# Delta-rule recurrence in 128-token chunks: another operand layout and another job order for the triangular inverse

## The chip, the cores and the metric

The kernel runs on one core of a Trainium2 chip. The time is device microseconds (us) of one execution; of several runs the median counts. The engines are PE (TensorE: matrix products, results to PSUM; PEld is its weight load), DVE (VectorE), ACT (ScalarE), POOL (GpSimd) and SP (DMA queues). Each works through its own instruction list in order and waits on semaphores where it needs another's result.

## What is computed

One encoder layer: an input projection feeds three head groups (an RWKV-7 mixer, a 2-D neighbourhood attention, a latent attention), then an output projection, layer norms and a feed-forward block. The change touches only the recurrence of the first group, for 1024 tokens, 4 heads of 64 channels, and two directions, each a scan over all tokens:

```python
def step(S, inp):
    r_t, w_t, k_t, v_t, a_t, b_t = inp
    sa = jnp.einsum('bhvk,bhk->bhv', S, a_t)
    S_new = S * w_t[:, :, None, :] + sa[..., None] * b_t[:, :, None, :] + v_t[..., None] * k_t[:, :, None, :]
    y = jnp.einsum('bhvk,bhk->bhv', S_new if inclusive else S, r_t)
    return S_new, y
y_fwd = wkv7_scan(rh, dec_h[:, :, 0], k_dir[:, :, 0], vh, -kk, kk * a_h[:, :, 0], True)
y_bwd = flip(wkv7_scan(flip(rh), flip(dec_h[:, :, 1]), ..., False))
```

## The kernel before

The scan is done in 8 chunks of 128 tokens (`i`), for both directions (`d`) and all four heads at once. In a chunk the rows of `sa` depend on each other through a triangular 128 x 128 matrix, so its inverse is needed. The inverse is built by doubling: blocks of 2 tokens are there at once, four levels (`m` = 1 to 4) make them 4, 8, 16 and 32 wide, and two last steps make 64 and 128.

The program is a list of jobs, `PLAN`, and PE, ACT and DVE each walk through it, doing their own part of every job. So the place in `PLAN` sets the order on three engines. The jobs of the inverse, `HOPS`, each depend on the one before:

- G, GT, D, E at each level: a product of the level's mask `Lev` with the inverse, its transpose, a product with the transposed inverse `Xt`, a transpose back. ACT copies the result of G, GT and D out of PSUM; after E, DVE adds it to the inverse (L1245) and transposes that (L1250).
- The inverse is held compactly: `Xc` has only the four 32 x 32 diagonal blocks (128 x 32 a head), `Xtc` the same transposed. At each level POOL makes the masked matrices `Lev` (L628) and spreads `Xtc` to a full block-diagonal `Xt` (L639), 128 x 512 elements each.
- G5, D5 join 32-blocks to 64-blocks (32 x 32 products), G6, D6 join 64 to 128 (64 x 64 products). They read full matrices `X` and `Xt`: after the fourth E, ACT copies the blocks of `Xc` into `X`, four copies a direction (L854), and DVE spreads `Xt` once more (L1253).

Between the hops stand the other jobs: A (the triangular matrix itself; for chunk i+1, behind G5 and D5), KR and R (other masked products of keys and queries), tok and V (transposes), AV and AZ (what values and the old state bring into the chunk, each 128 x 256, added on DVE), U (inverse times their sum), Y (the output), S (the new state). `BACK`, `FRONT` and `AHEAD` say after which hop each stands: AZ, U, Y and S of chunk i-1 in the first two levels of chunk i, then tok, V, KR, AV and R of chunk i. Level jobs use PSUM banks 4 to 7, the rest a ring of banks 0 to 3.

Names of jobs and lines on PE: A L1672, KR L1679, R L1684, G L1693, GT and E L1697, D L1702, G5 L1715, D5 L1718, G6 L1730, D6 L1733, tok L1738, V L1742, AV L1747, AZ L1755, U L1761, Y L1768 to L1774, S L1781 and L1782. On DVE: A L1232 to L1243, KR L1266, R L1271, D5 L1258 and L1259, D6 L1262, S L1283 and L1287, Y L1291. On ACT: A L846, G, GT and D L849, G5 L858, G6 L864, tok L866, V, AV and U L869.

## Time and profile before

| | |
|---|---|
| median of 3 runs | 1944.28 us (1942.8 to 1944.61) |
| profiled execution | 1947.11 us, span 1945.0 us |
| mean granted TensorE clock | 0.951 |
| PE busy | 1763.7 us, 91% of the span |
| DVE, ACT, POOL busy | 827.2, 555.5, 320.7 us |
| recurrence (first product at 745.2, last output added at 1061.7) | 316 us |
| one chunk in the middle of it | 37.55 us |

All rows are of the one profiled execution, in us from the start of its span. Busy PE includes time at the lower clock, so busy time is not a fixed amount of work. Products are pipelined: the time from one row's start to the next row's start says more than the duration in a row, which includes the way through the array.

### The profile page before, as it was taken

Reading aid. Unit: us, or ns where it says so; the run is one execution under the profiler, and the core shown is the slowest. Engines: PE = TensorE matmul, PEld = TensorE weight load, DVE = VectorE, ACT = ScalarE, POOL = GpSimd, SP = SyncE. Lnnn points to the kernel's source line nnn. Section 1 sums busy time; section 2 is a strip of 40 time slices with the busy share of each in tenths; the row PEclk is TensorE's granted clock in tenths of the full one; section 3 lists DMA queues with packets and bytes.
Section 4 is the critical chain, followed back from the end, with each engine's and each line's share of the span. In section 5 each row is a group of like instructions: output and inputs, shape, how many; then the busy total and the mean of one; then the engine's idle time right before and its main releaser. Section 6 shows DMA issues by size and latency. Waiting matters only on the chain.

```text
span 1945.0 us, 22750 instructions
## 1 busy us (share of the span) xinstructions
PE 1763.7 (91%) x8988; PEld 1261.4 (65%) x8988; DVE 827.2 (43%) x1193; ACT 555.5 (29%) x1058; POOL 320.7 (16%) x263
## 2 busy tenths in 40 slices
PE   2999978789999996888888997999999999999995
PEld 2888736544444433676676444888888888888884
DVE  7224348765534426545553646211211121133555
ACT  3111167734343322433432012111111111122331
POOL 1700011146000004455452015200000000000000
PEclk8999999989999997788887998999999999999998
DMA  4310000000000000000001300411111111144333
GB/s 187 130 54 32 11 29 1 12 5 4 8 4 4 0 0 14 2 2 2 2 2 53 153 11 11 152 43 43 52 56 43 43 51 57 56 149 138 95 95 115
DMA packets 24277, 93.49 MB, mean 48 GB/s; under 512 B 2752, under 2 KB 5120, under 8 KB 23568
## 3 DMA queue, kind: packets, MB, share of 16 engines
q1 hardware_dynamic: 23744, 87.27, 13.0%
q0 software_dynamic: 464, 5.28, 0.7%
q8 instruction: 46, 0.75, 0.2%
q14 instruction: 23, 0.19, 0.0%
HBM read 79.92 MB, written 12.58 MB: 48 GB/s over the span
## 4 chain that ended last, share of the span: by engine, by line
PE 84%; DVE 9%; ACT 4%; issue 2%; DMA 1%; POOL 0%; SPq 0%; DVEq 0%; ACTq 0%; POOLq 0%
PE psum L1842 25%; PE psum L1868 12%; PE psum L1456 9%; PE psum L1597 5%; PE psum L1793 5%; PE psum L1607 5%; PE psum L1474 2%; PE psum L1556 2%; PE psum L1538 1%; PE psum L1579 1%; PE psum L1693 1%; PE psum L1519 1%; PE psum L1481 1%; DVE stats L1138 1%; PE psum L1761 1%
## 5 line engine op out<-in xcount | busy, mean ns | idle before, releaser
L1842 PE MATMUL psum<-h_hi,w_hi 128*128 128x512 f32 x704 | 275.2, 391 | 11.7 <-DVE h_lo L1336 11.7
L1842 PE MATMUL psum<-h_lo,w_hi 128*128 128x512 f32 x704 | 274.4, 390 | 0.0
L1842 PE MATMUL psum<-h_hi,w_lo 128*128 128x512 f32 x704 | 274.4, 390 | 0.0
L1369 DVE TENSOR_TENSOR arena<-psum,arena 128x1024 f32 (+1 forms) x22 | 27.0, 1225 | 391.3 <-ACT arena L914 391.3
L1842 PEld LDWEIGHTS psum<-h_hi,w_hi 128*128 128x128 f32 x704 | 132.6, 188 | 39.7 <-DVE h_lo L1336 12.0
L1842 PEld LDWEIGHTS psum<-h_lo,w_hi 128*128 128x128 f32 x704 | 132.6, 188 | 27.8 <-issue 0.2
L1842 PEld LDWEIGHTS psum<-h_hi,w_lo 128*128 128x128 f32 x704 | 132.5, 188 | 27.5
L628 POOL TENSOR_TENSOR arena<-arena,consts 128x512 f32<-128x512 f32 x64 | 80.2, 1270 | 321.9 <-ACT arena L846 321.9
L1868 PE MATMUL psum<-wd_hi,act_lo 128*128 128x512 f32 x336 | 130.7, 389 | 0.0
L1868 PE MATMUL psum<-wd_lo,act_hi 128*128 128x512 f32 x336 | 130.7, 389 | 0.0
L1868 PE MATMUL psum<-wd_hi,act_hi 128*128 128x512 f32 x336 | 130.7, 389 | 0.0
L1138 DVE TENSOR_REDUCE stats<-psum 128x1 f32<-128x1024 f32 x64 | 78.0, 1224 | 122.8 <-PE psum L1579 122.8
L1597 PE MATMUL psum<-arena 97*128 97x512 f32 x256 | 121.4, 602 | 3.2 <-DMA arena<-arena 2.2
L1607 PE MATMUL psum<-arena 128*128 128x512 f32 x256 | 120.3, 592 | 0.0
L1793 PE MATMUL psum<-arena 128*128 128x512 f32 x256 | 110.6, 592 | 0.3 <-DMA arena<-in_w_out 0.3
L1382 DVE TENSOR_TENSOR wd_lo<-arena,wd_hi 128x1024 fp32r<-128x1024 f32 x44 | 53.9, 1225 | 129.8 <-ACT wd_hi L928 129.8
L1456 PE MATMUL psum<-h_hi,w_in_hi 128*128 128x512 f32 x240 | 96.5, 402 | 11.1 <-DVEq L999 11.1
L809 ACT ACTIVATE arena<-psum 128x1024 f32<-128x1024 f32 x64 | 65.4, 1022 | 133.4 <-PE psum L1597 133.4
L914 ACT ACTIVATE arena<-psum 128x1024 f32 (+1 forms) x22 | 22.6, 1027 | 273.9 <-PE psum L1842 273.9
L1456 PE MATMUL psum<-h_lo,w_in_hi 128*128 128x512 f32 x240 | 95.7, 399 | 0.0
L1456 PE MATMUL psum<-h_hi,w_in_lo 128*128 128x512 f32 x240 | 95.1, 396 | 0.0
L639 POOL TENSOR_TENSOR arena<-arena,consts 128x512 f32<-128x512 f32 x64 | 80.0, 1270 | 70.8 <-DVE arena L1250 53.6
(265 smaller groups left out, 2895.8 us busy)
## 6 DMA issues: line engine op xcount, KB each, us to landing
arena<-in_w_down SPq DMA_DIRECT2D x44, 512.0 KB, 3.6
arena<-in_w_gate SPq DMA_DIRECT2D x22, 512.0 KB, 3.5
arena<-in_w_up SPq DMA_DIRECT2D x22, 512.0 KB, 4.6
arena<-in_w_in SPq DMA_DIRECT2D x15, 512.0 KB, 3.6
arena<-in_x SPq DMA_DIRECT2D x8, 512.0 KB, 10.1
resid_spill<-arena POOLq DMA_DIRECT2D x1, 4096.0 KB, 12.9
arena<-in_w_out SPq DMA_DIRECT2D x8, 512.0 KB, 6.2
arena<-resid_spill SPq DMA_DIRECT2D x1, 4096.0 KB, 19.5
```

Source lines behind the costliest of these rows:

```text
L628: pool.tensor_tensor(Lev[d][m % 2], Araw[i % 2][d], four_heads(cst((C_LV if d == 0 else C_LVT) + m - 1)), ALU.mult).then_inc(lev_ready, 1)
L639: pool.tensor_tensor(Xt[d].rearrange("p h (k c) -> p h k c", c=32), spread(Xtc[d]), own_block, ALU.mult).then_inc(xt_full, 1)
L809: act.activation(halves(e_ring[(kt) % NE]), psum[:, 2 * (kt % 2):2 * (kt % 2) + 2, :], ACT.Exp, scale=MLA_SCALE).then_inc(e_ready, 1)
L1138: v.tensor_reduce(g_max[:, b, t:t + 1], psum[:, g_banks, :], AX.XY, ALU.max, negate=True).then_inc(g_max_ready, 1)
L1382: v.tensor_tensor(wd_lo[b], raw_w[b], wd_hi[b], ALU.subtract).then_inc(wd_lo_ready, 1)
L1456: mm = pe.matmul(bank(2 * b + hf), w[:, P * k:P * k + P], x[k][:, cols], start=(k == 0 and n == 0), stop=(k == KT - 1 and n == 2))
L1474: mm = pe.matmul(bank(t), x[k][:, t * P:(t + 1) * P], wv_parts[k // 2][:, HALF * (k % 2):HALF * (k % 2) + HALF], start=(k == 0 and n == 0) ...
L1597: mm = pe.matmul(bank(2 * (kt % 2) + hf), kT[b][0:97, kt * P:(kt + 1) * P], qT[b][0:97, hf * HALF:(hf + 1) * HALF], start=True, stop=True)
L1607: mm = pe.matmul(bank(6 + hf), vh[b][:, kt, :], e_ring[kt % NE][:, hf * HALF:(hf + 1) * HALF], start=(kt == 0), stop=(kt == NT - 1))
L1793: mm = pe.matmul(bank(mixed_bank(t) + hf), mix[:, k, t * P:(t + 1) * P], w_out[k][:, hf * HALF:(hf + 1) * HALF], start=(k == 2), stop=(k = ...
L1842: mm = pe.matmul(bank(4 * b + 2 * n + hf), w[b][n][:, P * k:P * k + P], x[k][:, cols], start=(k == 0 and i == 0), stop=(k == KT - 1 and i ...
L1868: mm = pe.matmul(bank(2 * t + hf), x[b][:, t * P:(t + 1) * P], w[b][:, hf * HALF:(hf + 1) * HALF], start=(free is not None and i == 0), st ...
```

## The change

Four things, in the recurrence alone.

1. G5 and D5 read the compact `Xc` and `Xtc` themselves. DVE's spreading for D5 (L1253) and ACT's four copies a direction (L854) are gone. `Xc` and `Xtc` exist twice, for even and odd chunks (`Xcs`, `Xtcs`).
2. The diagonal blocks that G6, D6 and U still need in full `X` and `Xt` are copied by POOL (`own_blocks`), 12 copies of 32 x 128 elements a chunk: four that G6 waits for, four that D6 waits for, four that U waits for.
3. G6 and D6 are one job each for both directions (`TOGETHER`), and PE alternates between the directions from product to product.
4. AV and AZ become one job AX that accumulates both in one PSUM bank; ACT copies the sum to `Xs`, and DVE's addition is gone. All jobs get other places (`BESIDE`; a "-" belongs to the chunk before, a "+" to the next). A of the next chunk stands in levels 1 and 2 now, at most one job stands after a hop.

```diff
-BACK = {0: ("AZ0", "AZ1"), 1: ("U0",), 2: ("U1",), 3: ("Y0",), 4: ("Y1",), 5: ("S0",), 6: ("S1",)}
-FRONT = {7: ("tok0",), 8: ("V0", "V1"), 9: ("tok1",), 10: ("KR0",), 11: ("KR1",), 12: ("AV0",), 13: ("AV1",), 14: ("R0",),
-         15: ("R1",)}
-AHEAD = {16: ("A0",), 17: ("A1",)}
+BESIDE = {0: ("R1-",), 1: ("tok0-",), 2: ("U1-",), 3: ("A1+",), 4: ("U0-",), 5: ("Y1-",), 7: ("A0+",), 8: ("Y0-",),
+          9: ("S0-",), 10: ("V0",), 11: ("KR1",), 12: ("S1-",), 13: ("V1",), 14: ("tok1",), 15: ("KR0",), 16: ("R0",),
+          17: ("AX1",), 18: ("AX0",)}
+TOGETHER = ("G6", "D6")
...
-    jobs = named(("A0", "A1"), 0)
-    for i in range(NT):
+    jobs = [("A", 0, 0, 0), ("A", 1, 0, 0)]
+    for i in range(NT + 1):
         for n, (kind, m) in enumerate(HOPS):
-            jobs += [(kind, d, m, i) for d in range(2)]
-            if i:
-                jobs += named(BACK.get(n, ()), i - 1)
-            jobs += named(FRONT.get(n, ()), i)
-            if i + 1 < NT:
-                jobs += named(AHEAD.get(n, ()), i + 1)
-    return jobs + named(("AZ0", "AZ1", "U0", "U1", "Y0", "Y1"), NT - 1)
+            if i < NT:
+                jobs += [(kind, d, m, i) for d in range(1 if kind in TOGETHER else 2)]
+            for name in BESIDE.get(n, ()):
+                j = i + name.count("+") - name.count("-")
+                kind_d = name.strip("+-")
+                if 0 <= j < NT and not (kind_d[0] == "S" and j == NT - 1):
+                    jobs.append((kind_d[:-1], int(kind_d[-1]), 0, j))
+    return jobs
...
-XT_AT = LEV_AT
-XTC_AT = {(d, m, i): 12 * i + 2 * (m - 1) + (1 + m // 4) * d + 1 for i in range(NT) for m in range(1, 5) for d in range(2)}
-OWN_AT = {(d, i): 12 * i + 2 * d + 8 for i in range(NT) for d in range(2)}
-TURNED_AT = {(d, i): 12 * i + d + 11 for i in range(NT) for d in range(2)}
+XT_AT = {(d, m, i): 20 * i + 2 * (m - 1) + d + 1 for i in range(NT) for m in range(1, 5) for d in range(2)}
+XTC_AT = {(d, m, i): 10 * i + 2 * (m - 1) + d + 1 for i in range(NT) for m in range(1, 5) for d in range(2)}
+TURNED_AT = {(d, i): 10 * i + d + 9 for i in range(NT) for d in range(2)}
+FIRST_HALF_AT = {i: 20 * i + 12 for i in range(NT)}
+TURNED_OWN_AT = {i: 20 * i + 16 for i in range(NT)}
+OTHER_HALF_AT = {i: 20 * i + 20 for i in range(NT)}
...
+        elif kind in TOGETHER:
+            banks[job] = (4 + turn[0], 6 + turn[1])
+            turn = [1 - turn[0], 1 - turn[1]]
...
-        Xc, Xtc, Gc, G5 = ([heads4(32) for d in range(2)] for _ in range(4))
+        Xcs, Xtcs = ([[heads4(32) for d in range(2)] for n in range(2)] for _ in range(2))
+        Gc, G5 = ([heads4(32) for d in range(2)] for _ in range(2))
...
-                        computed(pool, ("D6", d, 0, i - 1))
+                        computed(pool, ("D6", 0, 0, i - 1))
                 else:
                     pool.wait_ge(xt_ready, XTC_AT[d, m - 1, i])
-                pool.tensor_tensor(Xt[d].rearrange("p h (k c) -> p h k c", c=32), spread(Xtc[d]), own_block,
+                pool.tensor_tensor(Xt[d].rearrange("p h (k c) -> p h k c", c=32), spread(Xtcs[i % 2][d]), own_block,
                                    ALU.mult).then_inc(xt_full, 1)
 
+            def own_blocks(full, compact, which, i):
+
+                for d in range(2):
+                    pool.wait_ge(xt_ready, XTC_AT[d, 4, i])
+                    rows64 = halves_of(d)[which]
+                    for at in (rows64.start, rows64.start + 32):
+                        rows = slice(at, at + 32)
+                        pool.tensor_copy(full[d][rows, :, rows], compact[d][rows]).then_inc(xt_full, 1)
+
             for i in range(NT):
+                if i:
+                    pool.wait_ge(xt_full, OTHER_HALF_AT[i - 1])
                 for m in range(1, 5):
                     for d in range(2):
                         level(d, m, i)
                     for d in range(2):
                         turned_full(d, m, i)
+                pool.wait_ge(xt_full, XT_AT[1, 4, i])
+                own_blocks(X, Xcs[i % 2], 1, i)
+                own_blocks(Xt, Xtcs[i % 2], 0, i)
+                own_blocks(X, Xcs[i % 2], 0, i)
...
-                elif kind == "E" and m == 4:
-                    taken(act, job)
-                    for p in range(4):
-                        rows = slice(32 * p, 32 * p + 32)
-                        act.activation(X[d][rows, :, 32 * p:32 * p + 32], Xc[d][rows], ACT.Copy).then_inc(x_full, 1)
...
-                    dst, src = halves_of(d)
-                    ins = act.activation(G6[d][dst].rearrange("p h c -> p (h c)"), psum[dst, b0, 0:256], ACT.Copy)
+                    for d in range(2):
+                        dst, src = halves_of(d)
+                        ins = act.activation(G6[d][dst].rearrange("p h c -> p (h c)"), psum[dst, BANKS[job][d], 0:256], ACT.Copy)
...
+                    if i >= 2:
+                        v.wait_ge(xt_full, OTHER_HALF_AT[i - 2])
...
-                    if m == 4:
-                        v.wait_ge(xt_ready, XTC_AT[d, m, i])
-                        v.tensor_tensor(Xt[d].rearrange("p h (k c) -> p h k c", c=32), spread(Xtc[d]), own_block,
-                                        ALU.mult).then_inc(xt_ready, 1)
                 elif kind == "D5":
                     dst, src = quads(d, d)
-                    v.wait_ge(xt_ready, OWN_AT[d, i])
...
-                elif kind == "AZ":
-                    taken(v, ("AV", d, 0, i))
-                    v.tensor_tensor(Xs[d].rearrange("p h c -> p (h c)"), bank(b0, 256),
-                                    AVs[d].rearrange("p h c -> p (h c)"), ALU.add).then_inc(out_v, 1)
...
-                        pe.wait_ge(x_full, 4 * (2 * i + d + 1))
+                        taken(pe, ("E", d, 4, i))
                     else:
                         taken(pe, ("G5", d, 0, i))
-                        pe.wait_ge(xt_ready, OWN_AT[d, i])
+                        pe.wait_ge(xt_ready, XTC_AT[d, 4, i])
                     for p in range(2):
                         dst, src = quads(d, p)
                         for h in range(4):
                             out = psum[dst, banks[p], 32 * h:32 * h + 32]
                             if kind == "G5":
+                                mm = pe.matmul(out, Araw[i % 2][d][src, h, dst], Xc[d][src, h, :], start=True, stop=True,
+                                               skip_group_check=True)
+                            else:
+                                mm = pe.matmul(out, Xtc[d][dst, h, :], G5[d][dst, h, :], start=True, stop=True,
+                                               skip_group_check=True)
+                elif kind in TOGETHER:
+                    if kind == "G6":
+                        taken(pe, ("D5", 0, 0, i))
+                        taken(pe, ("D5", 1, 0, i))
+                        pe.wait_ge(xt_full, FIRST_HALF_AT[i])
+                    else:
+                        taken(pe, ("G6", 0, 0, i))
+                        pe.wait_ge(xt_full, TURNED_OWN_AT[i])
+                        pe.wait_ge(xt_ready, TURNED_AT[1, i])
+                    for h in range(4):
+                        for d in range(2):
+                            dst, src = halves_of(d)
+                            out = psum[dst, banks[d], 64 * h:64 * h + 64]
+                            if kind == "G6":
                                 mm = pe.matmul(out, Araw[i % 2][d][src, h, dst], X[d][src, h, src], start=True, stop=True,
                                                skip_group_check=True)
                             else:
-                                mm = pe.matmul(out, Xt[d][dst, h, dst], G5[d][dst, h, :], start=True, stop=True,
+                                mm = pe.matmul(out, Xt[d][dst, h, dst], G6[d][dst, h, :], start=True, stop=True,
...
-                elif kind == "AV":
+                elif kind == "AX":
                     taken(pe, ("KR", d, 0, i))
                     taken(pe, ("V", d, 0, i))
                     for h in range(4):
-                        mm = pe.matmul(psum[:, b0, 64 * h:64 * h + 64], KAm[d][:, h, :],
-                                       tokv[d][:, h // 2, 64 * (h % 2):64 * (h % 2) + 64], start=True, stop=True)
-                elif kind == "AZ":
+                        pe.matmul(psum[:, b0, 64 * h:64 * h + 64], KAm[d][:, h, :],
+                                  tokv[d][:, h // 2, 64 * (h % 2):64 * (h % 2) + 64], start=(h == 0), stop=False,
+                                  skip_group_check=True)
                     if i:
                         taken(pe, ("S", d, 0, i - 1))
                     else:
                         pe.wait_ge(y_cleared, 5)
                     for hp in range(2):
                         mm = pe.matmul(psum[:, b0, P * hp:P * hp + P], At[:, 2 * d + hp, at_chunk(d, i)], Zs[d][:, hp, :],
-                                       start=True, stop=True)
+                                       start=False, stop=True, skip_group_check=True)
                 elif kind == "U":
-                    taken(pe, ("D6", d, 0, i))
-                    taken(pe, ("AZ", d, 0, i))
+                    taken(pe, ("D6", 0, 0, i))
+                    pe.wait_ge(xt_full, OTHER_HALF_AT[i])
+                    taken(pe, ("AX", d, 0, i))```

What this makes of PE's list at the end of a chunk, from the last products of level 4 into the next chunk's first level. Before:

```order
L1702 MATMUL psum<-arena 32x128 x8
L1684 MATMUL psum<-arena 128x128 x4
L1697 MATMUL psum<-consts,arena 128x128 x2
L1684 MATMUL psum<-arena 128x128 x4
L1715 MATMUL psum<-arena 32x32 x16
L1672 MATMUL psum<-arena 128x128 x4
L1718 MATMUL psum<-arena 32x32 x16
L1672 MATMUL psum<-arena 128x128 x4
L1730 MATMUL psum<-arena 64x64 x8
L1733 MATMUL psum<-arena 64x64 x8
L1693 MATMUL psum<-arena 32x128 x8
L1755 MATMUL psum<-arena 128x128 x4
```

The same place after the change (L1715 is D, L1755 tok, L1710 E and GT, L1692 KR, L1728 G5, L1697 R, L1731 D5, L1764 and L1772 AX, L1747 G6, L1750 D6, L1706 G):

```order
L1710 MATMUL psum<-consts,arena 128x128 x2
L1692 MATMUL psum<-arena 128x256 x4
L1728 MATMUL psum<-arena 32x32 x16
L1697 MATMUL psum<-arena 128x128 x4
L1731 MATMUL psum<-arena 32x32 x16
L1764 MATMUL psum<-arena 128x64 x4
L1772 MATMUL psum<-arena 128x128 x2
L1747 MATMUL psum<-arena 64x64 x8
L1764 MATMUL psum<-arena 128x64 x4
L1772 MATMUL psum<-arena 128x128 x2
L1750 MATMUL psum<-arena 64x64 x8
L1706 MATMUL psum<-arena 32x128 x8
```

A KR now stands between E and G5, an R between G5 and D5, an AX before and after G6; the two A are gone from here.

PE's list in the first level and the start of the second, before (the AZ of both directions, then U, U, Y):

```order
L1693 MATMUL psum<-arena 32x128 x8
L1755 MATMUL psum<-arena 128x128 x4
L1697 MATMUL psum<-consts,arena 128x128 x2
L1761 MATMUL psum<-arena 128x64 x4
L1702 MATMUL psum<-arena 32x128 x8
L1761 MATMUL psum<-arena 128x64 x4
L1697 MATMUL psum<-consts,arena 128x128 x2
```

After (R, tok, U and A between the hops of level 1, then G of level 2 and a U; L1779 is U, L1685 A):

```order
L1706 MATMUL psum<-arena 32x128 x8
L1697 MATMUL psum<-arena 128x128 x4
L1710 MATMUL psum<-consts,arena 128x128 x2
L1755 MATMUL psum<-consts,arena 128x128 x4
L1715 MATMUL psum<-arena 32x128 x8
L1779 MATMUL psum<-arena 128x64 x4
L1710 MATMUL psum<-consts,arena 128x128 x2
L1685 MATMUL psum<-arena 128x128 x4
L1706 MATMUL psum<-arena 32x128 x8
L1779 MATMUL psum<-arena 128x64 x4
```

Each hop is followed by one other job, and the pair of AZ at its head is no longer there.

POOL's list after the change, at the turn from one chunk to the next (L631 is `Lev`, L642 the spreading to `Xt`):

```order
L631 TENSOR_TENSOR arena<-arena,consts 128x512 x2
L642 TENSOR_TENSOR arena<-arena,consts 128x512 x2
L652 COPY arena<-arena 32x4x32 x12
L631 TENSOR_TENSOR arena<-arena,consts 128x512 x2
L642 TENSOR_TENSOR arena<-arena,consts 128x512 x2
```

Before, the list had the same pairs without the copies; the next chunk's first `Lev` now comes after all twelve.

## Rows read from the trace of the kernel before

**Rows 1.** The page: busy time by engine; 40 slices of the span, TensorE's granted clock.

```profile
PE 1763.7 (91%) x8988; PEld 1261.4 (65%) x8988; DVE 827.2 (43%) x1193; ACT 555.5 (29%) x1058; POOL 320.7 (16%) x263
PEclk8999999989999997788887998999999999999998
```

**Rows 2.** Stretches (busy us and instructions, clock, DMA), then timeline of PE at G5.

```profile
1003.40:1041.00 37.60, 32.44 (x396) 25.78 (x396) 19.80 (x55) 15.08 (x51) 19.90 (x16) 0.86 0.01 2
...
778.10 0.56 PE L1715 MATMUL psum<-arena 32*32 32x32 f32 x16 [1.40 <-ACT arena L854]
...
1041.87 0.56 PE L1715 MATMUL psum<-arena 32*32 32x32 f32 x16 [1.40 <-ACT arena L854]
```

**Rows 3.** Timeline (start, duration, engine, line, [idle before <- releaser]), end of a chunk.

```profile
1002.56 0.28 DVE L1245 TENSOR_TENSOR arena<-psum,arena 128x128 f32<-128x128 f32 x1
1002.88 2.63 ACT L854 ACTIVATE arena<-arena 32x128 f32<-32x128 f32 x8 [1.27 <-DVE arena L1245]
...
1004.32 0.56 PE L1715 MATMUL psum<-arena 32*32 32x32 f32 x16 [1.41 <-ACT arena L854]
...
1005.65 0.56 PE L1715 MATMUL psum<-arena 32*32 32x32 f32 x16 [0.77 <-ACT arena L854]
...
1010.28 1.60 PEld L1730 LDWEIGHTS psum<-arena 64*64 64x64 f32 x16 [1.56 <-ACT arena L846]
1010.31 1.76 PE L1730 MATMUL psum<-arena 64*64 64x64 f32 x16 [1.29 <-DVE arena L1259]
```

**Rows 4.** Timeline of a middle chunk: G behind the state update, D behind POOL.

```profile
991.06 0.29 DVE L1245 TENSOR_TENSOR arena<-psum,arena 128x128 f32<-128x128 f32 x1
...
991.46 0.95 PE L1693 MATMUL psum<-arena 128*32 128x128 f32 x16 [0.88 <-ACT arena L866]
991.78 2.52 POOL L639 TENSOR_TENSOR arena<-arena,consts 128x512 f32<-128x512 f32 x2 [3.62 <-DVE arena L1250]
...
994.44 0.43 PE L1702 MATMUL psum<-arena 128*32 128x128 f32 x8 [0.28 <-ACT arena L866]
```

**Rows 5.** Stretches of the recurrence, columns as in rows 2 (the clock is third from last).

```profile
757.00:768.30 11.30, 10.86 (x97) 6.33 (x100) 2.18 (x8) 5.24 (x17) 11.23 (x10) 0.50 0.01 1
...
778.90:792.20 13.30, 11.76 (x126) 10.49 (x126) 8.21 (x24) 4.95 (x16) 6.88 (x6) 0.50 0.01 2
...
1007.30:1017.50 10.20, 8.90 (x88) 7.89 (x82) 6.40 (x20) 3.05 (x10) 6.75 (x6) 0.50 0.01 2
1017.50:1044.80 27.30, 23.34 (x320) 17.72 (x320) 13.59 (x35) 11.84 (x42) 13.16 (x11) 1.00 0.01 2
1045.00:1061.50 16.50, 15.90 (x97) 13.33 (x96) 3.16 (x9) 1.79 (x5) 0.00 (x0) 0.50 0.00 1
```

**Rows 6.** Timeline: A and AZ at the low clock, KR and AV at the full one.

```profile
1007.79 0.93 PEld L1672 LDWEIGHTS psum<-arena 64*128 64x128 f32 x8
1007.79 1.23 PE L1672 MATMUL psum<-arena 64*128 64x128 f32 x8
...
1014.75 1.78 PEld L1755 LDWEIGHTS psum<-arena 128*128 128x128 f32 x8 [0.38 <-ACT arena L849]
1014.76 2.08 PE L1755 MATMUL psum<-arena 128*128 128x128 f32 x8
...
1032.35 1.14 PE L1679 MATMUL psum<-arena 64*128 64x256 f32 x8
...
1036.00 1.10 PE L1747 MATMUL psum<-arena 128*128 128x64 f32 x8
```

**Rows 7.** Groups of POOL over the whole program, shapes apart (count | busy, mean ns).

```profile
L639 POOL TENSOR_TENSOR arena<-arena,consts 128x512 f32<-128x512 f32 x64 | 80.0, 1270 | 70.8 <-DVE arena L1250 53.6 <-PE psum L1733 15.9 <-DVE arena L1243 1.3
...
L590 POOL COPY arena<-arena 64x64 f32<-64x64 f32 x64 | 18.3, 286 | 98.4 <-PE psum L1519 96.4
```

**Rows 8.** Timeline at the end of the recurrence: the last U, the last output added.

```profile
1050.63 3.61 PE L1761 MATMUL psum<-arena 128*128 128x64 f32 x16
...
1061.24 0.42 DVE L1291 TENSOR_TENSOR arena<-psum,arena 128x256 f32<-128x256 f32 x1 [3.15 <-PE psum L1774]
```

45 lines of the change are left out of this document (17 added, 28 removed).

## The prediction

> **What bounds the kernel now.** The page first [rows 1]: TensorE (PE) is busy 91% of the span, and the clock line is below 9 tenths almost only in its slices 16 to 22. That is the recurrence, 745 to 1062 us: eight chunks, two directions at once. Next the table of stretches by chunk and PE's own rows [rows 2]: PE's first G5 starts at 778.10, the last at 1041.87, and the one before it at 1004.32 [rows 3]. So a chunk takes 37.55 us in the steady part, (1041.87 - 778.10) / 7 = 37.68 on average, and in a stretch of 37.6 us PE is busy 32.44, DVE 19.80, ACT 15.08, POOL 19.90. PE is the engine to look at: 32.4 us of work and 5.1 us of waiting. Everything the diff touches lies here; the other 1630 us stay.
>
> Where are the 5.1 us? In order of time [rows 3]: G5 waits 1.41 and 0.77 for the four ACT copies of the inverse (L854, 0.33 each), and G6 waits 1.29 for the DVE copy behind D5. That is 3.5. Earlier [rows 4] G waits 0.88 because the add L1245 before it starts late, at 991.06, right behind the state update L1283 and L1287 in DVE's list, and D waits 0.28; the row names ACT there, but the POOL pair L639 ends at the same 994.30 and D needs its second result. That is 1.2. The rest, about 0.5, is the "issue" idle before a product with other row groups.
>
> Where is PE's work dearer than it need be? In the clock [rows 5]. It is at the low level (0.50, 1.2 GHz) from 1007.3 to 1017.5 and at the full one from 1017.5 to 1044.8. It falls after G5, A and D5, small products with waits between them, stays low through G6 and D6, and comes back after G, the AZ products and the first U. All seven later chunks show this with 10.2 us of low clock, the first with 13.3 [rows 5]. In those 10.2 us PE is busy 8.9; at full clock the same work would take about half, so the low stretch costs 4.4 us a chunk.
>
> **The change part by part.** *Compact inverse for G5 and D5.* The eight ACT copies and the two DVE products L1253 leave; G5 needs only the add L1245 (0.28), D5 the transpose after it (0.31). With KR0 (1.14, as L1679 [rows 6]) placed between E and G5 the 1.41 and 0.77 are covered: **-2.2**. If KR0 did not cover it, 0.3 would come back. ACT loses 2.6 us and DVE 2.2, neither of them late elsewhere.
>
> *AX1 between D5 and G6, AX0 between G6 and D6.* AX is the AV product and the AZ product in one bank, so an ACT copy and a DVE add go too (both hidden already). AX lasts 1.0 (AV) and about 0.5 (half of what one direction's AZ took at the low clock), and nearly twice that at the low one [rows 6], longer than the 1.29 wait and than the evacuation of two G6 halves (2 x 0.38): **-1.3**. What is late next is DVE's R0 mask ahead of D5's four transposes and copies (2 us together); both fit under AX1.
>
> *Own blocks on POOL.* Twelve copies of 32 x 128 elements a chunk. The trace has no such copy. Nearest rows [rows 7]: a POOL copy of 64 elements took 0.286, a POOL product of 512 elements 1.27, so 0.29 to 1.27 each; I take 0.4, near the copy. G6 needs only the first four (1.6 us after E's transpose, while PE has 5 us of KR0, G5, R0, D5 and AX1 ahead of it): nothing. All twelve take 4.8; the two level masks of the next chunk (2 x 1.27), which ran beside D5 and G6 before, now follow, and then come the two L639, which wait for D6 as before. D in the first level needs the second L639, 2.5 us after D6, and PE gets there after G, R1, GT, tok0: 2.1 at full clock, 3.5 at the low one. I take a new wait of 0.3.
>
> *G6 and D6, both directions alternating.* The 16 instructions of G6 took 1.76 at the low clock, 0.11 apiece, and their weight loads 1.60 [rows 3]; D6 the same. Their operands lie in opposite row and column halves. What alternating halves brings is shown by A, whose products alternate the two row halves: 8 loads of 128 columns in 0.93 at low clock, where AZ's 8 full loads took 1.78 [rows 6]. So between nothing and half: 0 to -1.76 for both; I take **-1.1**, near A's own busy time per product (1.23 against 2.08).
>
> The Trainium skill bears on this. TensorEngine Tiling (Array Packing), Key Properties, says that different tiles can execute LdWeights and Matmul in parallel; its 64 x 64 table would make it the full -1.76, and the chunk 0.7 shorter than I say. G6 and D6 before did not gain from that, since their four heads in a row use the same tile.
>
> *Jobs spread.* A moves from the tail, where one cost 1.23 at the low clock, to levels 1 and 2; S0 and S1 leave level 2, where S1 held up the add: **-1.2** (the 0.88 and 0.28). New thin places: no job stands between D2 and E2 (D's product and its ACT copy need about 0.9 before E can start; 0.4 is open), V1 alone between GT4 and D4 (0.3), the second direction's G a little behind its add three times (0.4), and three more changes of row group (0.5). With the 0.3 above: **+1.9**. DVE's A job (two us) now stands ahead of Y1 and Y0 in DVE's queue; both products come over 2 us later, so nobody waits. On ACT, A's copy (0.60) stands ahead of G's copy, under U0 and Y0.
>
> *Clock.* The tail has still G5, R0, D5, which are thin, so I expect one fall a chunk, later than now, around AX1. Which work brings it back? Before it was G, AZ, GT and U in a row. Now it would be G, R1, GT, tok0, D of the next first level, packed almost as tightly (in the first chunk the low level ended at 768, after V, GT, tok and D [rows 5]). I take a low stretch between the 10.2 and the 13.3 of [rows 5]: **+0.8**.
>
> Sum for a chunk: -2.2 - 1.3 - 1.2 + 1.9 - 1.1 + 0.8 = -3.1, so 34.4 us in place of 37.55.
>
> Over the program: seven periods, 7 x -3.1 = -21.7. The A jobs sit in the chunk before their own, so the last period is 1.3 shorter, and the first chunk saves its G5 wait but gets two A jobs: 0. After the last G5, now 19.8 us [rows 8] nearly all at the low clock, there are now also R0, R1, the AV part twice and a tok0 that nobody uses: +5.9 at that clock; G6/D6 and waits give back 2.4: +3.5. In all -19.5. Against the profiled execution's 1947.1 (span 1945.0) that is 1927.6; the median shown is 1944.3, 2.8 lower, so **1925**.
>
> **The rivals.** *The clock stays low through levels 1 and 2 (slower).* For it: after the last chunk PE is busy 15.9 of 16.5 us with AZ, U and Y and the clock is 0.50 all through [rows 5]; U's and Y's are just the jobs that now fill levels 1 and 2, and AZ's burst, after which the clock returned, is gone. Against it: G, R1, GT, tok0 and D stand before them. If the clock comes back only between level 3 and S0, the low stretch is 12 to 16 us longer. A low microsecond costs 4.4 / 10.2 = 0.43, so that is +5 to +7 a chunk, a chunk of 39.5 to 41.5, and 1959 to 1972. It turns the sign once the low stretch is over about 18 us.
>
> *The clock does not fall.* For it: no wait of PE in the chunk is over 0.5 us any more. Then the 4.4 and the 0.8 go, G6/D6 save only half of 1.1, and a chunk is near 30; at the end some 3 more: 1893.
> By the Trainium skill (TensorE: Matmul & The Clock Gate, the HAM clock gate) idleness throttles the clock and activity releases it; read as idleness alone, this is its case. The row against it: D6 and G ran nearly without a gap and the clock stayed low [rows 3, 5], though PE hardly idled there.
>
> *POOL becomes the bound.* If a copy costs over 0.55, the next chunk's masks and L639 come after PE; each further 0.1 is 1.2 us a chunk, and at 0.8 the gain is gone. At 1.27 a chunk would be 43 and the time 1985.
>
> *The gain is there but mostly given back*, some chunks with an early and some with a late return of the clock, or the covers thinner than I count: a chunk of 36 to 37.6, 1936 to 1947.
>
> **How the numbers follow.** My forecast (chunks of 33.5 to 35.5, 1913 to 1934) 0.50; no fall of the clock 0.13; mostly given back 0.15; low through two levels 0.17; POOL 0.05. The range must leave out no more than 0.2: from 1892, the case of no fall, to 1955, past the given-back case and up to the late return's near end; my forecast's own is 1913 to 1934. A measurement here can tell about 0.2%, 4 us, from no change: faster is 0.50 + 0.13 + 0.09 = 0.72, within it 0.07, slower 0.21.
>
> **What would show it.** Right: G5 rows without a wait for ACT, G6's wait for D5's copy gone, G6 plus D6 at 2.4 us or less for 32 instructions, DVE's A rows in levels 1 and 2, G5 to G5 at 34 to 35. The granted clock by stretch decides: one low stretch of 10 to 14 us that ends before U1 is my case; low until S0 or KR1 is the slower rival. POOL: COPY rows near 0.4 and L639 (now L642) starting just after D6. It would be wrong if those start late, or if PE's idle time in a chunk is over 3 us.

## The result, and the profile after

| | before | after |
|---|---|---|
| median | 1944.05 us (1942.8 to 1944.61, 4 runs) | 1872.72 us (1872.56 to 1874.17, 4 runs) |
| span of the profiled execution | 1945.0 us | 1870.7 us |
| G5 to G5 in the steady part | 37.6 us | 28.6 us |
| mean granted clock | 0.951 | 0.972 |

The ratio is 0.9636, 95% interval 0.9619 to 0.9652. The kernel is 71 us faster, where the forecast was 19; the time lies 19 us below the low end of the range, 1892.

The page of after, the lines that answer to [rows 1]:

```profile
PE 1722.4 (92%) x8988; PEld 1224.1 (65%) x8988; DVE 824.8 (44%) x1161; ACT 534.1 (29%) x994; POOL 348.7 (19%) x359
PEclk8999999989999998899999998999999999999998
```

There are as many products on PE as before, in 41 us less of busy time, while the whole is 74 us shorter. The dip of the clock line in slices 16 to 22 is two slices long now. The stretches of the recurrence, to be read beside [rows 2, 5] (us, then busy us and instructions of PE, PEld, DVE, ACT, POOL, then the granted clock):

```profile
741.10:765.00 23.90, 13.91 (x122) 7.92 (x122) 16.13 (x45) 6.22 (x19) 14.89 (x12) 0.53 0.01 1
...
858.30:886.90 28.60, 27.82 (x399) 21.59 (x397) 19.41 (x51) 12.22 (x42) 23.41 (x28) 1.00 0.01 2
...
972.60:986.70 14.10, 13.67 (x198) 11.68 (x196) 6.78 (x15) 4.49 (x13) 3.17 (x12) 1.00 0.01 2
```

The clock is low once in the recurrence, at its start (0.53 in the first stretch shown), and full from 766.2 to the end of the recurrence: **it does not fall in any chunk.** PE idles 0.8 us in a chunk of 28.6; before it was 5.1 in 37.6.

The timeline of the end of a chunk in after answers to [rows 3] and, for POOL, to [rows 7]:

```profile
858.28 0.89 PE L1728 MATMUL psum<-arena 32*32 32x32 f32 x32
859.11 0.71 PE L1697 MATMUL psum<-arena 64*128 64x128 f32 x8
859.75 0.93 PE L1731 MATMUL psum<-arena 32*32 32x32 f32 x32
860.61 1.10 PE L1764 MATMUL psum<-arena 128*128 128x64 f32 x8
861.55 0.66 PE L1772 MATMUL psum<-arena 128*128 128x128 f32 x4
862.20 0.68 PE L1747 MATMUL psum<-arena 64*64 64x64 f32 x16
862.81 1.10 PE L1764 MATMUL psum<-arena 128*128 128x64 f32 x8
...
867.83 0.43 PE L1715 MATMUL psum<-arena 128*32 128x128 f32 x8 [0.42 <-ACT arena L880]
...
874.72 0.52 PE L1710 MATMUL psum<-consts,arena 128*128 128x128 f32 x2 [0.27 <-ACT arena L867]
...
886.59 4.08 POOL L652 COPY arena<-arena 32x128 f32<-32x128 f32 x12 [2.28 <-DVE arena L1265]
```

G5 (L1728), R0 (L1697), D5 (L1731), AX1 (L1764, L1772), G6 (L1747) and AX0 follow one another without a wait: from the start of G5 to the start of D6 (L1750, 864.35) it is 6.1 us. Twelve POOL copies take 4.08, 0.34 each from start to start. What is left of waits are the two predicted small ones, D behind POOL's second product (0.42; the row names ACT, POOL's L642 ends at 867.69) and E behind D (0.27).

Where the 74.3 us of span came from: the recurrence starts at 743.26 instead of 745.2 (1.9); first A to first G5 29.2 instead of 32.9 (3.7); seven periods 200.1 instead of 263.8 (63.6); last G5 to the last output add 14.1 instead of 19.8 (5.7); the rest is 0.6 the other way.

### The profile page after: what moved, and what is told of

Read it like the earlier page. It is cut to its first block, busy times and chain, and to the rows that moved or that the text cites. A ratio compares the mean times of both kernels' runs of the same rounds, so it can differ in the third digit from the quotient of the medians.

```text
span 1870.7 us, 22729 instructions
## 1 busy us (share of the span) xinstructions
PE 1722.4 (92%) x8988; PEld 1224.1 (65%) x8988; DVE 824.8 (44%) x1161; ACT 534.1 (29%) x994; POOL 348.7 (19%) x359
## 3 DMA queue, kind: packets, MB, share of 16 engines
q1 hardware_dynamic: 23744, 87.27, 13.7%
## 4 chain that ended last, share of the span: by engine, by line
PE 87%; DVE 8%; ACT 3%; issue 1%; DMA 1%; SPq 0%; POOL 0%; DVEq 0%; ACTq 0%; POOLq 0%
PE psum L1860 26%; PE psum L1886 12%; PE psum L1468 9%; PE psum L1609 6%; PE psum L1811 6%; PE psum L1619 5%; PE psum L1486 2%; PE psum L1568 2%; PE psum L1550 2%; PE psum L1591 2%; PE psum L1531 1%; PE psum L1493 1%; PE psum L1710 1%; DVE stats L1152 1%; PE psum L1706 1%
## 5 line engine op out<-in xcount | busy, mean ns | idle before, releaser
L631 POOL TENSOR_TENSOR arena<-arena,consts 128x512 f32<-128x512 f32 x64 | 80.9, 1285 | 265.4 <-ACT arena L864 264.8
L1811 PEld LDWEIGHTS psum<-arena 128*128 128x128 f32 x256 | 48.3, 190 | 63.7 <-issue 59.3
```

Of the source, the lines that this page charges most:

```text
L631: pool.tensor_tensor(Lev[d][m % 2], Araw[i % 2][d], four_heads(cst((C_LV if d == 0 else C_LVT) + m - 1)), ALU.mult).then_inc(lev_ready, 1)
L1811: mm = pe.matmul(bank(mixed_bank(t) + hf), mix[:, k, t * P:(t + 1) * P], w_out[k][:, hf * HALF:(hf + 1) * HALF], start=(k == 2), stop=(k = ...
```

## The experiments

The **theory** after the result: two parts of about equal size. The waits go, as predicted, and with them goes the fall of the clock, which they had caused. The **rival**: most of the gain is order and waits, and the clock only follows. A second question is which part of the change carries it. "Period" below is G5 to G5 and "low" the time per chunk at 0.50, both in the one profiled execution. Each run has its own runs of before beside it. "Run 4" is the one told under 4.

| kernel | median, us | ratio (95%) | period | low |
|---|---|---|---|---|
| before | 1944 to 1947 | 1 | 37.6 | 10.2 |
| before, waits filled | 1957.6 | 1.0043 to 1.0085 | 38.0 to 40.4 | 3.4 to 10.2 |
| before, waits covered | 1970.4 | 1.0118 to 1.0156 | 41.0 | 17.1 |
| after, before's places | 1986.0 | 1.0142 to 1.0237 | mostly 43.5 | 20.5 |
| after, ACT copies | 1923.9 | 0.9857 to 0.9911 | 34.5 (once 35.8) | 10.2 (once 13.7) |
| after, R moved | 1905.0 | 0.9760 to 0.9813 | 29.2 to 33.3 | 0, 6.8 or 10.2 |
| after, R and KR moved | 1908.6 | 0.9779 to 0.9834 | 29.6 to 33.9 | 0, 6.8 or 10.2 |
| R moved, four products | 1896.8 | 0.9732 to 0.9762 | 30.9 | 0 |
| R moved, one product | 1886.3 | 0.9676 to 0.9742 | 29.6 | 0 |
| after, not alternating | 1877.9 | 0.9643 to 0.9675 | 29.1 | 0 |
| **after** | **1872.7** | 0.9619 to 0.9652 | 28.6 | 0 |
| after, short head | 1872.3 | 0.9609 to 0.9635 | 28.6 | 0 |
| after, warm head | 1886.7 | 0.9678 to 0.9706 | 28.6 | 0 |

**1. Filling before's waits.** The kernel before with throw-away products (128x128 by 256 columns, results unused) meant for its three waits at the end of a chunk, three ahead of the first G5, two ahead of the second, three ahead of G6:

```diff
                     if kind == "G5":
+                        filler(b0, 3 - d)
                         pe.wait_ge(x_full, 4 * (2 * i + d + 1))
...
                     if kind == "G6":
+                        if d == 0:
+                            for before in PREVIOUS["AZ", 0, 0, i]:
+                                taken(pe, before)
+                            filler(BANKS["AZ", 0, 0, i][0], 3)
```

> The kernel before with throw-away TensorE products (128x128 by 128x256, about 0.43 us each at full clock) put into its three waits: three ahead of G5 of direction 0, two ahead of direction 1, three ahead of G6. Nothing of the real work is moved or removed; no result is used. Theory 'clock': the low stretch of 10.2 us in each chunk comes from the waits and small products between level 4 and G6; with the waits filled the clock stays at the full level, a chunk goes from 37.55 to about 33 us (4.4 us less), the time to about 1909 (1900 to 1915). Rival 'waits': the time went with the waits themselves, the clock is a side effect; here all waits stay, so 1944 or up to 10 more.

It is slower, not faster. PE's timeline in it, and two rows of DVE (L1232 is A's, L1259 D5's):

```profile
935.90 1.24 DVE L1232 TENSOR_TENSOR arena<-psum,consts 32x128 f32<-32x128 f32 x4 [1.03 <-ACT arena L846]
935.91 0.71 PE L1677 MATMUL psum<-arena 64*128 64x128 f32 x8
938.18 0.28 DVE L1259 COPY arena<-psum 32x128 f32<-32x128 f32 x1
938.56 2.90 PE L1660 MATMUL psum<-consts 128*128 128x256 f32 x6 [1.94 <-DVE arena L1259]
941.39 1.60 PE L1740 MATMUL psum<-arena 64*64 64x64 f32 x16
```

The filler at G5 did its work: G5, A and D5 ran at the full clock. That ahead of G6 (L1660) filled nothing. G6 writes the bank that D5 wrote, the program waits for that bank before it comes to the filler, and the bank is free only after D5's copy (938.18 to 938.46); the filler's own bank, A's, had been read by 937.14. So all 1.94 us of G6's wait stand ahead of the filler, the clock fell in that wait (937.7), and 2.9 us of products at the low clock then stood ahead of G6. The run does not decide: the kernel before with all three waits filled was never run. It shows that with the two waits at G5 filled the one at G6 still lets the clock fall. It also gives a price. In three of its periods the low stretch is 10.2 us, in three 3.4, with the same products; they take 40.2 to 40.4 and 38.0 to 38.2, some 0.32 us for each low microsecond.

**2. The new places without the compact operands.** The kernel before with KR0, R0 and the two AV jobs between the steps, as the changed kernel has them:

```diff
-FRONT = {7: ("tok0",), 8: ("V0", "V1"), 9: ("tok1",), 10: ("KR0",), 11: ("KR1",), 12: ("AV0",), 13: ("AV1",), 14: ("R0",),
-         15: ("R1",)}
+FRONT = {7: ("tok0",), 9: ("tok1",), 10: ("V0",), 11: ("KR1",), 13: ("V1",), 14: ("R1",), 15: ("KR0",), 16: ("R0",),
+         17: ("AV1",), 18: ("AV0",)}
```

> The kernel before with another table of places only: KR0 behind E of level 4, R0 behind G5, AV1 behind D5, AV0 behind G6; A stays behind G5 and D5 (it has to, with one Xc and Xtc), AZ stays in the next level 1, the ACT copies stay. Theory 'clock': the waits of 1.4, 0.8 and 1.3 are covered and PE has real work there, the clock does not fall, a chunk is 37.55 - 3.3 - 4.4 = 30 us: about 1888 (1880 to 1900). Rival 'waits': only the 3.3 us go, 34.3 a chunk, about 1920. A third, that the compact operands are what does it: 1930 or more, since G5 still waits for ACT.

```profile
936.15 0.29 DVE L1219 TENSOR_TENSOR arena<-arena 128x128 f32<-128x128 f32 x1
936.36 0.28 DVE L1245 TENSOR_TENSOR arena<-psum,arena 128x128 f32<-128x128 f32 x1
...
938.10:979.10 41.00, 35.81 (x396) 28.45 (x397) 19.96 (x55) 15.53 (x51) 19.80 (x16) 0.79 0.01 1
...
979.12 0.84 PE L1715 MATMUL psum<-arena 32*32 32x32 f32 x16 [2.17 <-ACT arena L854]
```

(Two rows of DVE ahead of G5, the stretch of one chunk, and PE's next first G5.) G5 waits 2.17 for ACT's copies, more than the 1.41 of before, and the clock falls there; what was put behind, R, AV and A, now runs at the low clock. The wait is longer through this table itself. It puts R1 ahead of the last E, and R1's work on DVE is a mask, a reciprocal and a product (L1271, L1217, L1219); the add L1245, from which ACT copies, stands behind them and starts at 936.36, 1.5 us after E's product was out (934.88). So this table costs 25 us without the compact operands; what KR0 and R0 at G5 would have done without R1's move no run shows.

**3. The compact operands without the new places.** The changed kernel with the jobs where before had them:

```diff
-BESIDE = {0: ("R1-",), 1: ("tok0-",), 2: ("U1-",), 3: ("A1+",), 4: ("U0-",), 5: ("Y1-",), 7: ("A0+",), 8: ("Y0-",),
-          9: ("S0-",), 10: ("V0",), 11: ("KR1",), 12: ("S1-",), 13: ("V1",), 14: ("tok1",), 15: ("KR0",), 16: ("R0",),
-          17: ("AX1",), 18: ("AX0",)}
+BESIDE = {0: ("AX0-", "AX1-"), 1: ("U0-",), 2: ("U1-",), 3: ("Y0-",), 4: ("Y1-",), 5: ("S0-",), 6: ("S1-",),
+          7: ("tok0",), 8: ("V0", "V1"), 9: ("tok1",), 10: ("KR0",), 11: ("KR1",), 14: ("R0",), 15: ("R1",),
+          16: ("A0+",), 17: ("A1+",)}
```

> The changed kernel with the places of before: AX of both directions, U, Y, S of the chunk before in levels 1 and 2, R and nothing else around level 4's end, A of the next chunk behind G5 and D5. Compact operands, POOL copies, alternating G6/D6 stay. Theory 'clock': PE idles again between E, G5, D5 and G6 and the clock falls each chunk: 28.6 + 4.4 + about 1.5 of waits = 34.5 a chunk, about 1915 (1905 to 1925). Rival 'operands': the compact feed and the alternating products keep the clock up without the places; 31 a chunk or less, 1892 or less.

```profile
950.50:970.90 20.40, 16.63 (x124) 14.65 (x126) 5.79 (x19) 4.13 (x13) 10.40 (x11) 0.50 0.01 2
...
947.05 1.08 PE L1728 MATMUL psum<-arena 32*32 32x32 f32 x32
...
953.11 1.12 PE L1747 MATMUL psum<-arena 64*64 64x64 f32 x16 [2.86 <-DVE arena L1269]
955.39 1.12 PE L1750 MATMUL psum<-arena 64*64 64x64 f32 x16 [1.17 <-ACT arena L878]
```

G5 has no wait, but G6 waits 2.86 (D5's copies stand behind A's job in DVE's list) and D6 1.17, and the clock stays low for 20.5 us. This is the slower rival's price by another trigger: in the two forms tried, the places without the compact operands and these without the places, the kernel is 25 and 41 us **slower** than before, together they are 71 faster. The two forms are not clean halves: run 2 leaves A behind G5 and D5 and has R1 ahead of E, run 3 keeps the alternation and AX.

**4. The alternation alone.**

```diff
-                    for h in range(4):
-                        for d in range(2):
+                    for d in range(2):
+                        for h in range(4):
```

> The changed kernel with the two loops of G6 and D6 exchanged, so that four heads of one direction follow each other in one tile. Theory 'clock': the clock is not touched; 16 instructions at full clock go from 0.61 us to half of the 1.76 of before, 0.88, so +0.27 twice a chunk, +4.3 in all: about 1877 (1875 to 1880). Rival: the alternation is part of what holds the clock up: low stretches return and it is 1900 or more. Second rival: it brings nothing, 1872.7.

```profile
859.60:888.70 29.10, 28.33 (x398) 22.12 (x396) 19.38 (x51) 12.23 (x42) 23.39 (x29) 1.00 0.01 2
...
863.50 0.82 PEld L1747 LDWEIGHTS psum<-arena 64*64 64x64 f32 x16
863.53 0.93 PE L1747 MATMUL psum<-arena 64*64 64x64 f32 x16
```

(The stretch of a chunk, then G6.) In after the last two rows are

```profile
862.17 0.57 PEld L1747 LDWEIGHTS psum<-arena 64*64 64x64 f32 x16
862.20 0.68 PE L1747 MATMUL psum<-arena 64*64 64x64 f32 x16
```

0.25 to 0.27 us for each of G6 and D6, 0.5 a chunk, 5.2 us in all (1877.9 against 1872.7).

**5. ACT's copies back, places kept.** ACT copies the inverse into a full matrix, and G5 reads that; POOL copies only the transposes:

```diff
+                elif kind == "E" and m == 4:
+                    taken(act, job)
+                    for p in range(4):
+                        rows = slice(32 * p, 32 * p + 32)
+                        act.activation(X[d][rows, :, 32 * p:32 * p + 32], Xcs[i % 2][d][rows], ACT.Copy).then_inc(x_full, 1)
...
-                        taken(pe, ("E", d, 4, i))
+                        pe.wait_ge(x_full, 4 * (2 * i + d + 1))
```

> Edit: the changed kernel with the compact feed of G5 alone undone: ScalarE copies the four diagonal blocks of each direction's inverse into a full matrix behind E's last evacuation, G5 reads that matrix, POOL copies only the transposes. The places of all fills, the alternating loops and the second set of compact buffers stay. Theory 'the operands give the wait, the places give the clock': G5 waits again about 1.5 us a chunk for the copies (in the kernel with only the places moved it waited 2.17 and 0.48), the granted clock stays full, period about 28.6 + 1.5 = 30.1, time 1872.7 + 7 x 1.5 + 1.5 = 1885 (1880 to 1892). Theory 'the wait at G5 is itself what lowers the clock, since behind it stand only products on part of the array': the clock falls in each chunk as in the kernels with periods of 37.6 to 43.5, period 37 to 42, time 1930 to 1970.

```profile
811.20:845.70 34.50, 32.51 (x396) 25.69 (x397) 18.97 (x51) 14.77 (x51) 21.14 (x21) 0.85 0.01 3
...
848.30:858.50 10.20, 10.20 (x106) 9.03 (x107) 2.73 (x7) 2.42 (x8) 1.11 (x2) 0.50 0.01 2
...
845.71 0.56 PE L1733 MATMUL psum<-arena 32*32 32x32 f32 x16 [0.82 <-ACT arena L871]
847.03 0.56 PE L1733 MATMUL psum<-arena 32*32 32x32 f32 x16 [0.77 <-ACT arena L871]
```

The waits are 0.82 and 0.77, 1.59 as the first theory said, but the period grew by 5.9: the other 4.3 are the 10.2 us at the low clock. The second theory was right in kind and too dear in size (1930 or more). The second row also shows what a fall is like: PE has not one idle tenth in those 10.2 us, and the clock is low all the same.

**6. R moved away from between G5 and D5.** R0 (0.64 us) goes to the next chunk's second level; no work is added or removed:

```diff
-15: ("KR0",), 16: ("R0",),
+15: ("KR0",), 6: ("R0-",),
```

> Edit: the changed kernel with the rows of direction 0's R (8 products, 0.64 us) taken from behind G5 to behind G1 of the next chunk, so that nothing stands between G5 and D5. No work is added or left out. Theory 'clock': what is lost is the wait of D5 for G5's evacuation on ScalarE, about 0.5 us a chunk, plus what the clock does: if it stays full, period 29.1 and 1877; if the tail of the chunk (G5 to D6) is then too empty and it falls in each chunk, period 36 or more and 1925 or more. Theory 'waits alone' (the kernel's gain is its covered waits, the clock only follows the load of the whole recurrence): 1877 and no stretch at half the clock behind the first.

```profile
807.70:837.00 29.30, 28.21 (x399) 21.58 (x398) 19.84 (x51) 12.39 (x42) 23.45 (x28) 1.00 0.01 3
837.00:869.10 32.10, 31.25 (x399) 24.21 (x397) 20.33 (x51) 12.49 (x42) 23.40 (x28) 0.89 0.01 2
...
841.00:847.80 6.80, 6.80 (x68) 5.79 (x66) 0.84 (x2) 2.03 (x6) 4.18 (x4) 0.50 0.01 2
...
838.24 1.13 PE L1731 MATMUL psum<-arena 32*32 32x32 f32 x32 [0.38 <-ACT arena L871]
```

This run prices the clock by itself. The first two rows are two neighbouring chunks of one execution: the same 399 products, 1.1 and 0.9 us idle, one with the clock full and one with 6.8 us of it low, and the second is 2.8 us longer: 0.41 us for each low microsecond (the prediction had 0.43). New are a wait of 0.38 ahead of D5 and R0's absence there; five of seven periods had a fall, two had none. In the profiled execution 19.4 of the 34.1 us that it is slower than after lie in the seven periods, 11.7 behind the last G5, where the clock is low for 27.3 us, and 3.0 ahead of the first.

**7. KR0 moved too**, so that G5 as well has nothing ahead of it:

```diff
-12: ("S1-",), 13: ("V1",), 14: ("tok1",), 15: ("KR0",), 16: ("R0",),
+12: ("S1-",), 13: ("V1", "KR0"), 14: ("tok1",), 6: ("R0-",),
```

> Edit: as the run with R moved, and KR of direction 0 (0.64 us) moved from in front of G5 to behind D4's place 13, in front of the last alternation of D4 and E4. G5 then starts as soon as POOL has copied the block it reads or waits for it. Theory 'clock': two holes in the tail (ahead of G5 about 0.5 to 1.2 us, behind it 0.5), the granted clock falls to half in most chunks, period 37 to 42, time 1930 to 1970. Theory 'waits alone': period 28.6 + 1.0 to 1.7 = 29.6 to 30.3, time 1880 to 1886, the clock full throughout.

Waits of 0.37 at G5 and 0.16 at D5; a fall in all but one period, 6.8 or 10.2 us long. It falls nearly always, as the first theory has it, but such a chunk takes 32.1 to 33.9 and not 37 to 42; the time is that of run 6 within 4 us. (G5 waits for the add behind E, not for a POOL copy as the expectation says: it reads the compact matrix.)

**8. Run 6 with something in R's old place.** Four throw-away products behind G5, then, in another kernel, one:

```diff
+                        if d == 0:
+                            for before in PREVIOUS["AX", 1, 0, i]:
+                                taken(pe, before)
+                            filler(BANKS["AX", 1, 0, i][0], 4)
                         taken(pe, ("G5", d, 0, i))
```

> Edit: the run with R moved (1905.0 us; chunks with a low stretch of the clock take 31.5 to 33.3 us, the two without 29.2 and 29.3), and added between G5 and D5, where R stood, four throw-away products of 128x128 by 256 columns of constants into columns of a bank that nothing reads. It only adds work to TensorE. Theory 'clock': the hole behind G5 is what lets the clock fall there, and filled with anything it doesn't fall, or in fewer chunks; periods 29.1 to 29.5, time 1876 to 1882 (faster than without the products by 23 to 29 us, although work was added). Theory 'waits and order': R's new place costs what it costs, the products add 0 to 0.5 us a chunk, time 1905 to 1909, low stretches as before.

> Edit: as the run with R moved and four throw-away products behind G5 (1896.8 us, period 30.9, no low stretch, the products 1.65 to 1.99 us a chunk), but with one such product (0.41 to 0.5 us a chunk), somewhat less than the 0.64 us of R that stood there in the changed kernel. The product starts 0.3 us behind G5 as the four did and ends before G5's evacuation is there or 0.3 us after it. Theory 'clock, and what stands behind G5 carries it': the clock stays full, period 29.2 to 29.5, time 1877 to 1880. Theory 'clock, and one product isn't enough there': low stretches in some or all chunks as without any (1905.0), period 31 to 33, time 1895 to 1906. Theory 'order and waits' (the four products helped by something else than the clock): 1905 or more.

The stretch of a chunk with four, and with one; then PE with one:

```profile
837.70:868.60 30.90, 29.88 (x407) 22.88 (x405) 19.85 (x51) 12.32 (x42) 23.43 (x29) 1.00 0.01 2
```

```profile
802.80:832.40 29.60, 28.56 (x401) 21.74 (x399) 19.84 (x51) 12.32 (x42) 23.43 (x29) 1.00 0.01 3
...
802.82 0.90 PE L1737 MATMUL psum<-arena 32*32 32x32 f32 x32
804.04 0.70 PE L1672 MATMUL psum<-consts 128*128 128x256 f32 x2 [0.33 <-ACT arena L871]
804.67 0.89 PE L1740 MATMUL psum<-arena 32*32 32x32 f32 x32
```

Work was added, and the kernel is faster than run 6 by 8 us with four products and by 19 with one: in the profiled executions no chunk has a low stretch any more. The rival falls here: nothing else in these rows could turn added work into a gain. And the product does not fill the wait. D5 writes the banks that G5 wrote, so the program waits for G5's copies (ACT L871) before it comes to the product; PE waits 0.33 there, where it waited 0.38 in run 6. The wait has stayed and the fall has gone. So a wait of this length does not make the clock fall by itself; in run 6 it falls with the wait and with G5 and D5 alone around it, and here 0.6 us of full-width work behind the wait is enough to hold it.

Against the full-clock chunks of run 6, 29.2 and 29.3, four products add 1.6 us and one adds 0.3; that is why four give less. Both times are worse than expected (1876 to 1882, 1877 to 1880). Four take 1.92 us from the first's start to D5, one takes 0.63. And one is near the edge: its four executions took 1883.4, 1884.0, 1888.6 and 1895.7 us, and the mean granted clock of the last is 0.964 where the profiled one has 0.972. That is an estimated 30 us more at the low level, or 12 us of time at 0.41, as much as it is slower; some chunks must have had their fall again, which no trace shows. The four executions with four products lie within 0.8 us, at 0.972 each.

**9. The start of the recurrence.** Four of five clears of matrices are moved from ahead of the first A's job on VectorE to behind it, and the last chunk's tok0, which nothing reads, is left out; then, in another kernel, there are besides throw-away products in the three waits of the start. The edit of the clears:

```diff
-            for ap in (y_out, *Zs, *X):
-                v.memset(ap, 0.0).then_inc(y_cleared, 1)
-            v.wait_ge(y_cleared, 5)
+            v.memset(Zs[0], 0.0).then_inc(y_cleared, 1)
...
+                    if d == 1 and i == 0:
+                        for ap in (Zs[1], *X, y_out):
+                            v.memset(ap, 0.0).then_inc(y_cleared, 1)
```

> Edit: the changed kernel; at the recurrence's start only the one matrix that is read first is cleared ahead of the first A, the other four clears (each on VectorE) come behind A's own job of chunk 0, and the last chunk's tok of direction 0, which nothing reads, is left out. Periods are untouched (28.6 at full clock). Theory 'the head is a chain through VectorE': the first A starts sooner by the four clears it no longer waits for, 2 to 4 us, time about 1869 (1867 to 1872). Theory 'the head is hidden behind the loads or the cumulative products': 1872 to 1873, no difference. If the clock's low stretch at the start (741 to 765) stays longer because of the emptier start: up to 1875.

> The kernel of the run with the short head, in five rounds beside the warm start and on the same chip. First A to first G5 took 25.3 us there, 29.2 in the changed kernel, but the loads and projections ahead of the first A ended 1.5 us later in the profiled execution. If that delay is chance: 1872.7 - 3 = 1869 to 1870, ratio 0.961. If the head's chain only waits elsewhere for the time it has gained: 1872 to 1873, ratio 0.963.

> Edit: the run with the short head (period 28.6; the only low stretch of the clock in the recurrence is the 20.5 us at its start, 744 to 764), and throw-away products on TensorE in the three waits of the start: 10 ahead of the first A, 40 ahead of chunk 0's first G of direction 0, 8 ahead of that of direction 1. Theory 'clock': the granted clock does not fall at the start, the PE-bound stretch from the first G to the first G5 (some 15 us busy at half the clock) shortens by 2 to 4 us, time 1869 to 1871. Theory 'the start is POOL's' (POOL is busy 4.9 of 5 us there): the clock may stay full, but the first G5 comes at most 1 us sooner, time 1872. Against both: if the clock falls all the same, the 40 products take 10 us instead of 5 and the start is later by 2 to 5 us, 1875 to 1878.

The short head took the stretch from A to the first G5 from 29.2 to 25.6 us, but the first A came at 744.7 and 745.5 in its two profiled executions where it was 743.3 in after, so of the 3.6 us 1.3 are left in the span (1869.3 and 1869.4), and 1872.7 and 1872.3 us are not measurably below after's 1872.7. The warm head kept the clock full:

```profile
747.00:768.80 21.80, 21.80 (x115) 18.36 (x113) 7.07 (x16) 1.06 (x3) 7.57 (x6) 1.00 0.00 1
768.80:786.20 17.40, 13.75 (x172) 7.88 (x168) 9.76 (x30) 8.35 (x28) 12.54 (x11) 1.00 0.00 1
```

but the 40 products ahead of the first G took 17.5 us, 3.5 times the 5 that I had given them, and pushed it back by some 15. From direction 1's first G to the first G5 it is 17.9 us at the full clock and 19.1 and 19.35 in the two short heads, so products of the right size could have given 1.2 to 1.4. No version was found that beats the changed kernel by more than a measurement can tell.

## Why the prediction was wrong

The direction was right and the size was a quarter of it. By its own steps, a chunk:

| step | predicted | measured |
|---|---|---|
| G5 and G6 covered (KR0, AX1) | -3.5 | -3.5, no wait in either |
| G's 0.88 and D's 0.28 | -1.2 | -1.2, both gone |
| new waits and row-group changes | +1.9 | +0.4 (idle 5.1 before, 0.8 now) |
| G6/D6 alternating | -1.1 at the low clock | -0.5 at the full one (run 4) |
| clock | +0.8 | -4.1 (PE busy 32.44 before, 28.33 in run 4) |
| sum | -3.1 | -8.9, measured -9.0 |

**The step that failed is "one fall a chunk, later than now".** It kept a cost whose cause the steps before had taken away. The clock in before fell at 1007.3, after waits of 1.41 and 0.77 between small products [rows 3, 5]; the third wait, G6's 1.29, came only after the fall, though run 1 shows that it makes the clock fall where the two before it are filled. I removed all three, named none in their place above 0.5, and still let the clock fall because G5, R0 and D5 "are thin". They are near the edge: with 1.59 us of waits at G5 the fall is there in every chunk (run 5), without R0 in most (run 6). But R0 was counted on the wrong side. With it the clock holds, and run 8 shows that it is R0's work and not the 0.38 us that it covers: another product behind the same wait does as well. I had looked at R0 and KR0 as covers for a wait only. This step (+0.8 for -4.1) is 4.9 of the 5.8 us a chunk that I missed; the new waits are 1.5, and the alternation takes 0.6 back.

The row that I held against the rival "the clock does not fall" was that D6 and G ran without a gap and the clock stayed low. Run 5 repeats it (10.20 busy of 10.20 at 0.50), but it speaks of how long a fall lasts, not of what starts one. The two are different questions, and I used one row for both. In the Trainium skill, TensorE: Matmul & The Clock Gate, the HAM clock gate, the clock is throttled by default and activity releases it. These runs agree in part: longer waits brought the fall (run 5) and added work took it away (run 8). But a wait of 0.33 us alone does not bring it, and in run 5 PE shows as busy through the whole low stretch.

**Its case was in the list, and too small.** "Near 30" for a chunk and 1893: right in kind, given 0.13. It was 20 us short: about 10 in the periods (28.6, not 30), 6 at the end, 5 to 6 ahead of the first G5, where I had said 0, less 1.3 for a last period that did not get shorter (28.54: PE waits 1.5 us in it). By the prediction's own terms this case comes to 1889 to 1891, a little under the 1893 that it names. The new waits were summed at 1.9 from single guesses of 0.3 to 0.5 (only the wait of D1, 0.4, and one of E behind D, 0.3, were real). And the end was put at +3.5 from work at the low clock; without the fall it is -5.7, 14.1 us at 1.00 where before had 19.8 nearly all at 0.50 [rows 5].

**Alternation.** At half the clock G6 took 1.76 before; the full clock alone makes it 0.88, the alternation 0.61 from start to start (862.20 to 862.81). Run 4 gives 0.87 (863.53 to 864.40). So 0.26 of 0.87 is saved, 30%, and my middle value was 31% (1.1 of 3.52); the row of A from which I argued was of the right size. The Trainium skill, TensorEngine Tiling (Array Packing), Key Properties, says that different tiles can execute LdWeights and Matmul in parallel; the half that I had worked out from it was not reached.

**Right:** POOL's copies (0.34 each, forecast 0.4), the wait of D1 for L642 (0.4, forecast 0.3), no one waiting for DVE's A job, POOL not the bound (busy 23.4 of 28.6, though it is now the next after PE).

**The slower rival** priced a low clock through levels 1 and 2 at 39.5 to 41.5 a chunk. It did not occur. Runs 2 and 3 stand there or beyond, at 41.0 and 43.5, with 17.1 and 20.5 us low, but their waits are longer too (5.2 and 6.8 us idle a chunk), so they do not test the turning point of "over about 18 us".

**A reading that was off.** In before six chunks have a low stretch of 10.2 us, not seven: the first has 13.7 and the last 20.5, to the end of the recurrence and beyond.

**Open.** Why two of run 6's chunks escaped the fall, with rows alike in every instruction and wait, is not settled; the start of a low stretch does not stand at one fixed product, but 2.6 to 4.0 us behind G5 in that run. How little work in R0's place still holds the clock is open too: with one product it mostly does. Which of U's, A's or G's products brings the clock back was not tried by itself.

## What to carry to other kernels

When a change removes the waits that stand ahead of a fall of the clock, price the fall as gone first, and as kept only if waits are left there with nothing but small products around them; a low microsecond cost 0.41 here (0.32 in run 1). An independent job between two dependent small products can be worth more than the wait it covers: R0 covers 0.38 us a chunk and was worth 32 us in all. Try such a change whole, since parts of it can each be slower than nothing. If no real work is at hand, one throw-away product is cheap (0.6 us), but price it from a row of its own kind, and look which wait the program comes to first: the fillers at G6 and at D5 both stood behind the wait that they were meant to fill.

## What the runs showed that was not expected

- The fall is a matter of a few tenths: with 0.64 us of work taken from between G5 and D5, and a wait of 0.38 in its place, low stretches of 6.8 or 10.2 us came in five of seven periods; with the work there, none in seven.
- A low stretch goes on while the profile shows PE busy all the time (10.20 of 10.20, run 5), and longer where waits recur in it: 10.2, 17.1 and 20.5 us in runs 5, 2 and 3.
- With one product of 128x128 by 256 columns, 0.6 us, behind a wait of 0.33 at that place the clock falls in no chunk of the profiled execution (run 8); the slowest of the four shows a lower mean clock.
- Sixteen fp32 products of 64x64 by 64 columns take 0.61 us alternating between opposite row and column halves, 0.87 when four in a row use the same.
